# A hybrid attention and mLSTM layer: turned rows of q and k moved to GpSimd's DMA queue through DRAM, two separate scale broadcasts, softmax steps placed first, four split blocks of x kept in DRAM

## Chip, cores and metric

One core of one Trainium2 chip. The metric is the device time of one execution in microseconds (us). Before the change three executions took 2060.83, 2059.70 and 2060.79 us, median 2060.79 us. TensorE is called PE, VectorE DVE, ScalarE ACT, GpSimd POOL and SyncE SP, as in the profile.

## What is computed

```python
h = rmsnorm(x, norm_w); proj = h @ w_in            # x is 1024 x 2048, w_in 2048 x 9232, float32
q_a,k_a,v_a,z_a, q_m,k_m,v_m,o_m,z_m, g = split(proj)
# group A, 8 heads x 128: q and k are normalised (rmsnorm), their first 32 dims rotated,
# out[:, :16] = x1*cos - x2*sin, out[:, 16:32] = x2*cos + x1*sin
# three dilated windows (128,1), (512,4), (2048,16), mixed by their softmax denominators
attn = sum_p mix_p * softmax(q k^T / sqrt(128) + mask_p) v ; attn *= silu(z_a)
# group B, 4 heads, qk 128, v 256: chunkwise mLSTM forward and backward, summed, normalised
hm = sigmoid(o_m) * rmsnorm(h_fwd + h_bwd) * silu(z_m)
return x + concat(attn, hm) @ w_out
```

## The kernel before

**The products.** Every float32 operand is split into a high and a low part (`t_hi`, `t_lo` of x; `w_hi`, `w_lo` of the weights), and each product is three matmuls: high by high (L714), low by high (L716), high by low (L718); in the output projection they are L742, L743 and L744. The input projection is done by a Strassen-like scheme with seven products for a group of two 128-column weight tiles, two halves of the 1024 tokens and half of the 2048 inputs. The seven left operands, products 0 to 6, are sums of four quarter blocks of x (B11, B12, B22, B21), each 512 tokens by 512 inputs as 128 partitions x 2048 numbers, held split in `t_hi[:, n]` and `t_lo[:, n]`.

**The unit.** The program is written as units `u`. One unit is one product: 12 matmuls of 128 x 512. Units 0 to 447 are the input projection (64 groups of 7), units 448 to 575 the output projection. Every engine runs one loop over `u` and in each unit does, in order: the eviction of unit u-1 (DVE L1204 to L1217, ACT L969 and L974), the split of the weights of unit u+2 (ACT `w_hi` L961, DVE `w_lo` L1190), then whatever other work is placed at that unit, and last the sums of weight blocks (`s_tmp`, DVE L1225 to L1246). PE does the unit's product first, then the small matmuls that are placed there. All queues are in order, SP's too: a `wait_ge` on SP holds all loads and stores behind it.

**The blocks of x.** The x blocks are built three times, because the input half (1024 of the 2048 rows) changes: at unit 0 (half 0), around unit 105 (half 1) and around unit 329 (half 0 again). `BUILD_AT[2]` is unit 329. A build loads the four quarters (`x_block`, L390), ACT scales them with the norm weight (L983), DVE makes four sums (`t_one`, `t_three`, `t_two`, `t_four`, L1254 to L1272), and for each of the seven products ACT writes the high part (`t_high`, L1003) and DVE the low part (`t_low`, L1281). These come at offsets 1, 3, 4, 5, 6, 8 and 9 from `BUILD_AT[b]` for products 0, 2, 1, 3, 4, 6 and 5. The product n of the new half is first used in unit 336 + n.

**The attention heads.** Head h starts at `A_START[h]` = 357 + 18 h; `at` is the unit counted from there. A head's steps:

- at -4: SP loads q and k (`raw_a`, `raw_b`) from the projection's result in DRAM (`fin`).
- at 0 to 3: squares (ACT), column sums (PE L863), root and reciprocal; SP stores the scales to `rs_dram` (at 3).
- at 2: SP loads the 32 rotated rows of q and k once more as 128 partitions x 256 (`turn`, L531, eight transfers). at 4 and 5: DVE rotates them (`rotate`, L1531 to L1540; it signals `a_rot`).
- at 5 on SP: wait for the scales, then two broadcasts of them into `a_q` and `a_k` (L543, 512 KB each). at 5 and 6 on SP: wait for `a_rot`, then four transfers SBUF to SBUF that put the turned rows back into `raw_a` or `raw_b` (L550).
- at 6: SP loads z (L556). at 8: SP waits for the normalised q, then loads v into `raw_a` (L560).
- DVE: at 7 normalised q (`normed`, L1547), at 8 z times the row scale (L1581), at 9 normalised k, at 10 v times the row scale (L1584).
- at 10 to 21: eight softmax steps, each with scores on PE (L894), masking and minimum on DVE (`masked`, L1559, L1564), exponentials on ACT (L1092), reciprocal on DVE (L1570), normalisation on ACT (L1098), transposes on PE (L911), copies out of PSUM (ACT L1105, DVE L1620) and values (PE L925, L929).

The steps of one head from at 18 on lie in the same units as the first steps of the next head. Heads 5, 6 and 7 lie in the output projection, where DVE also adds the residual and frees the PSUM bank (`output`, L1635). In groups 48 to 63 the projection's results are added to what the first half left in DRAM, by POOL's accumulating DMAs (L364 to L376). POOL does nothing else after unit 39.

Of the kernel before, what the change touches and what calls it, by code (L numbers as in the profile page):

```python
# [7 lines left out]
F32 = mybir.dt.float32  # L8
# [83 lines left out]

def chunk_of(n):
    return n if n < TB else STEPS - 1 - n
# [14 lines left out]
def build_program(nc, xT, w_all, w_gates, vecs, norm_cols, m_cols, att_mask, rope, eye, tri, fin, part, y_dram, eps_dram, rows_dram, rs_dram,  # L109
                  outT):  # L110
    with ExitStack() as ctx:
# [85 lines left out]
        turn = [view(4096, 512), view(4608, 512)]  # L197
        eps_rows, qk_rs = tri_m[:, 0, :], tri_m[:, 1, :]
# [46 lines left out]
        b_in = [[sem(f"b_in{i}_{k}") for k in range(KP)] for i in (B11, B12, B22)]  # L245
        b21_in = sem("b21_in")
# [3 lines left out]
        tl_done = [sem(f"tl_done{n}") for n in range(PRODUCTS)]  # L250

# [12 lines left out]
        x_ss = sem("x_ss")  # L264
        x_rms = sem("x_rms")
        x_rs = sem("x_rs")
        x_cols = sem("x_cols")
        x_bc = sem("x_bc")
        x_norm = sem("x_norm")
        eps_out = sem("eps_out")  # L270
# [44 lines left out]
        bc_in = sem("bc_in")  # L315
        turn_in = [sem(f"turn_in{i}") for i in range(2)]
        a_rot = sem("a_rot")
# [9 lines left out]
        a_mh = sem("a_mh")  # L327
# [54 lines left out]
        def _(sp):  # L382
# [4 lines left out]
            def x_block(b, blk, kt):  # L387
# [3 lines left out]
                             ).then_inc(b21_in if blk == B21 else b_in[blk][kt], 16)  # L391
# [37 lines left out]
            def gate_stores(u):  # L429
                if u == 48:  # L430
                    sp.wait_ge(x_cols, 6)
                    sp.dma_start(eps_dram, spread1[0:2 * TB, 0, :]).then_inc(eps_out, 16)
# [4 lines left out]

            def build_loads(b, off):
                if off == -13:
                    if b == 1:  # L440
                        sp.wait_ge(g_pe, 1)
                        sp.wait_ge(rows_out, 64)
# [6 lines left out]
                for blk, at in ((B11, -13), (B12, -12), (B22, -11), (B21, -9)):  # L449
                    if off == at:  # L450
                        for kt in range(KP):
                            x_block(b, blk, kt)

            def mlstm_loads(j, at):
                g = M_FINAL[j]
                n, odd = divmod(at - 18, 2)
                if odd == 0 and 0 <= n < STEPS:
# [3 lines left out]
                    else:  # L461
                        sp.wait_ge(eps_out, 16)
                        sp.wait_ge(rows_out, 64)
# [40 lines left out]
            def attention_loads(h, at):  # L504
                g = A_FINAL[h]
                if at == -4:
                    if h == 0:
                        sp.wait_ge(tl_done[1], t_made(1, 2))
                        sp.wait_ge(tl_done[5], t_made(5, 2))
                        sp.wait_ge(tl_done[3], t_made(3, 2))  # L510
                        sp.wait_ge(tl_done[4], t_made(4, 2))
                        sp.wait_ge(tl_done[6], t_made(6, 2))
                        sp.wait_ge(m_t, 16 * M_HEADS)
                        sp.dma_start(eps_rows[0:2 * TB], eps_dram).then_inc(eps_out, 16)
# [1333 lines left out]
```

## Time and profile before

| | |
|---|---|
| median of three executions | 2060.79 us |
| the profiled execution's own time | 2060.51 us |
| its span, first to last instruction | 2058.4 us |
| PE busy | 1990.4 us, 97% of the span |
| DVE, ACT, POOL busy | 1300.3, 848.7, 174.0 us |
| DMA | 281.53 MB, mean 137 GB/s |
| mean granted TensorE clock | 0.993 |

The profile is one execution. Busy time of PE counts pipelined matmuls until their modelled end. "Idle before" a group is the engine's idle time just before its instructions, put down to what ended it. PEq and SPq are the sequencers.

### The profile page before, as it was taken

Reading aid. Unit: us, or ns where it says so; the run is one execution under the profiler, and the core shown is the slowest. Engines: PE = TensorE matmul, PEld = TensorE weight load, DVE = VectorE, ACT = ScalarE, POOL = GpSimd, SP = SyncE. Lnnn points to the kernel's source line nnn. Section 1 sums busy time; section 2 is a strip of 40 time slices with the busy share of each in tenths; the row PEclk is TensorE's granted clock in tenths of the full one; section 3 lists DMA queues with packets and bytes.
Section 4 is the critical chain, followed back from the end, with each engine's and each line's share of the span. In section 5 each row is a group of like instructions: output and inputs, shape, how many; then the busy total and the mean of one; then the engine's idle time right before and its main releaser. Section 6 shows DMA issues by size and latency. Waiting matters only on the chain.

```text
span 2058.4 us, 27134 instructions
## 1 busy us (share of the span) xinstructions
PE 1990.4 (97%) x9257; PEld 1626.8 (79%) x9257; DVE 1300.3 (63%) x2669; ACT 848.7 (41%) x1350; POOL 174.0 (8%) x156
## 2 busy tenths in 40 slices
PE   4999999999999999999998999999989999999999
PEld 3887788788888888888887878778777787778887
DVE  7777757768768768768778566575665544433222
ACT  5553325335335426335454253644536344242110
POOL 4340000110010010010000111010110000000000
PEclk9999999999999999999999999999999999999999
DMA  4552335564474465375354655364555625425443
GB/s 160 182 179 88 109 113 184 121 151 123 118 166 119 116 161 144 97 180 141 98 199 108 158 138 132 75 154 93 113 121 158 233 66 170 141 74 184 144 153 107
DMA packets 160551, 281.53 MB, mean 137 GB/s; under 512 B 18288, under 2 KB 39312, under 8 KB 160160
## 3 DMA queue, kind: packets, MB, share of 16 engines
q1 hardware_dynamic: 141984, 246.25, 37.3%
q0 software_dynamic: 18432, 33.56, 11.6%
q8 instruction: 75, 1.23, 0.2%
q14 instruction: 60, 0.49, 0.1%
HBM read 185.23 MB, written 92.41 MB: 135 GB/s over the span
## 4 chain that ended last, share of the span: by engine, by line
PE 87%; DVE 4%; issue 3%; ACT 2%; DMA 2%; SPq 1%; DVEq 0%; ACTq 0%
PE ps L714 18%; PE ps L718 18%; PE ps L716 18%; PE ps L742 5%; PE ps L743 5%; PE ps L744 5%; PE ps L925 3%; PE ps L894 2%; PE ps L863 1%; PE ps L819 1%; PE ps L828 1%; PE ps L911 1%; PE ps L822 1%; PE ps L929 1%; DVE w_lo L1190 1%
## 5 line engine op out<-in xcount | busy, mean ns | idle before, releaser
L714 PE MATMUL ps<-t_hi,w_hi 128*128 128x512 f32 x1792 | 717.5, 400 | 48.3 <-DVE t_lo L1644 12.4
L716 PE MATMUL ps<-t_lo,w_hi 128*128 128x512 f32 x1792 | 702.0, 392 | 0.0
L718 PE MATMUL ps<-t_hi,w_lo 128*128 128x512 f32 x1792 | 701.9, 392 | 0.0
L714 PEld LDWEIGHTS ps<-t_hi,w_hi 128*128 128x128 f32 x1792 | 338.8, 189 | 130.5 <-issue 64.1
L718 PEld LDWEIGHTS ps<-t_hi,w_lo 128*128 128x128 f32 x1792 | 338.7, 189 | 72.3
L716 PEld LDWEIGHTS ps<-t_lo,w_hi 128*128 128x128 f32 x1792 | 339.4, 189 | 65.8
L961 ACT CAST w_hi<-w_raw 128x512 fp32r<-128x512 f32 x256 | 158.4, 619 | 417.6 <-PE ps L718 200.8
L961 ACT CAST w_hi<-s_tmp 128x512 fp32r<-128x512 f32 x256 | 158.6, 620 | 268.2 <-PE ps L718 239.6
L1190 DVE TENSOR_TENSOR w_lo<-s_tmp,w_hi 128x512 fp32r<-128x512 f32 x256 | 182.3, 712 | 125.2 <-ACT w_hi L961 115.7
L1190 DVE TENSOR_TENSOR w_lo<-w_raw,w_hi 128x512 fp32r<-128x512 f32 x256 | 181.7, 710 | 119.9 <-ACT w_hi L961 113.5
L742 PE MATMUL ps<-t_hi,w_hi 128*128 128x512 f32 x384 | 155.7, 405 | 9.5 <-DVE xt L1635 9.5
L743 PE MATMUL ps<-t_lo,w_hi 128*128 128x512 f32 x384 | 151.4, 394 | 0.0
L744 PE MATMUL ps<-t_hi,w_lo 128*128 128x512 f32 x384 | 151.0, 393 | 0.0
L1635 DVE TENSOR_TENSOR xt<-ps,s_tmp 128x512 f32<-128x512 f32 x64 | 43.9, 687 | 142.8 <-PE ps L744 142.8
L364 POOL DMA_DIRECT2D fin_dram<-xt x32 | 27.8, 869 | 911.2 <-ACT xt L974 911.2
L742 PEld LDWEIGHTS ps<-t_hi,w_hi 128*128 128x128 f32 x384 | 73.3, 191 | 30.2 <-issue 15.9
L744 PEld LDWEIGHTS ps<-t_hi,w_lo 128*128 128x128 f32 x384 | 73.1, 190 | 15.9
L743 PEld LDWEIGHTS ps<-t_lo,w_hi 128*128 128x128 f32 x384 | 73.5, 191 | 14.0
L1054 ACT ACTIVATE arena<-arena,g_cols 128x128 f32<-128x128 f32 x64 | 25.8, 403 | 131.6 <-DVE arena L1427 131.6
L969 ACT COPY xt<-ps 128x512 f32<-128x512 f32 x64 | 37.6, 587 | 96.6 <-PE ps L718 96.5
L1092 ACT ACTIVATE arena<-arena,mins 128x704 f32<-128x704 f32 x64 | 56.6, 884 | 43.1 <-DVE mins L1564 43.0
L1098 ACT ACTIVATE arena<-arena,sums 128x704 f32<-128x704 f32 x64 | 56.4, 882 | 43.2 <-DVE sums L1570 43.2
(215 smaller groups left out, 2667.6 us busy)
## 6 DMA issues: line engine op xcount, KB each, us to landing
w_raw<-w_all_dram SPq DMA_DIRECT2D x320, 256.0 KB, 3.6
fin_dram<-xt SPq DMA_DIRECT2D x128, 256.0 KB, 4.2
fin_dram<-xt POOLq DMA_DIRECT2D x128, 256.0 KB, 4.5
arena<-fin_dram SPq DMA_DIRECT2D x64, 512.0 KB, 6.4
arena<-xT_dram SPq DMA_DIRECT2D x48, 256.0 KB, 5.8
arena<-xT_dram SPq DMA_DIRECT2D x16, 512.0 KB, 4.0
arena<-rs_dram SPq DMA_DIRECT2D x16, 512.0 KB, 5.9
y_raw<-y_dram SPq DMA_DIRECT2D x16, 512.0 KB, 5.1
```

Source lines behind the costliest of these rows:

```text
L714: nc.tensor.matmul(ps[:, bank, :], hi, t_hi[:, n, k, :], start=new and k == 0, stop=False, skip_group_check=True)
L716: nc.tensor.matmul(ps[:, bank, :], hi, t_lo[:, n, k, :], start=False, stop=False, skip_group_check=True)
L718: mm = nc.tensor.matmul(ps[:, bank, :], lo, t_hi[:, n, k, :], start=False, stop=k == KP - 1, skip_group_check=True)
L742: nc.tensor.matmul(ps[:, half, :], hi, yh, start=piece == 0 and k == 0, stop=False)
L743: nc.tensor.matmul(ps[:, half, :], hi, yl, start=False, stop=False)
L744: mm = nc.tensor.matmul(ps[:, half, :], lo, yh, start=False, stop=piece == 1 and k == KP - 1)
L925: nc.tensor.matmul(out, vtok[:, 4 * h + b, :], pT[:, b, :], start=b == 0, stop=False)
L961: nc.scalar.copy(w_hi[:, b % 3, :], src).then_inc(hi_done, 1)
L1092: nc.scalar.activation(prob[:, i % 2, 0:KEYS], prob[:, i % 2, 0:KEYS], ACT.Exp, bias=mins[:, i % 2:i % 2 + 1], scale=-1.0, accum_out=sums[ ...
L1098: nc.scalar.activation(prob[:, i % 2, 0:KEYS], prob[:, i % 2, 0:KEYS], ACT.Copy, scale=sums[:, 2 + i % 2:3 + i % 2]).then_inc(a_p, 1)
L1190: nc.vector.tensor_tensor(w_lo[:, b % 3, :], src, w_hi[:, b % 3, :].bitcast(F32), ALU.subtract).then_inc(lo_done, 1)
L1635: nc.vector.tensor_tensor(xt[:, e % 6, :], ps[:, e % 2, :], s_tmp[:, e % 3, :], ALU.add).then_inc(o_done, 1)
```

## The change

What it does, part by part:

1. **Turned rows.** The rotated rows of q and k are written to a new DRAM tensor `rot_dram` and read back into `raw_a` / `raw_b`, both on POOL's queue: one store (128 KB) and one load (128 KB) each for q and k instead of four SBUF-to-SBUF transfers on SP. POOL waits for `a_rot`, stores, and waits for the store's semaphore `rot_out` before it loads. The order of the 32 dims is interleaved (`TURNED`), so `turn` is loaded by four transfers instead of eight, and the shuffle mask becomes `r ^ 2`.
2. **Scales.** The broadcasts of q's and k's scales go out at 5 and at 6 with a semaphore each (`bc_in[i]`), and `normed` waits only for its own.
3. **v and z.** v gets a place of its own (`v_at`), its load moves from at 8 to at 4 and no longer waits for the normalised q. On DVE v is scaled at 7 (before: 10), q normalised at 8 (7), k at 9 (9), z scaled at 10 (8).
4. **Softmax steps first.** On DVE and ACT the head's softmax steps come at the start of a unit, ahead of the eviction and the weight split.
5. **Kept blocks.** Products 1, 3, 4 and 5 (`KEPT`) of the first build are stored to `t_dram` by SP in units 16 to 44 (eight stores of 1 MB) and loaded back in units 332 to 336 (eight loads of 1 MB). The third build then makes only products 0, 2 and 6: no load and no scaling of B12, none of the four sums, no high and low parts of the four.
6. **Semaphores.** B12, B22 and B21 wait for all four pieces of a quarter; several others are merged.

```diff
+KEPT = (1, 3, 4, 5)
+        v_at = view(5504, 1024)
 # SP
+            def t_stores(u):
+                i, rest = divmod(u - 16, 8)
+                if rest in (0, 4) and 0 <= i < len(KEPT):
+                    n = KEPT[i]
+                    sp.wait_ge(tl_done[n], t_made(n, 0))
+                    sp.dma_start(t_dram[i, rest // 4], flat_t((t_hi, t_lo)[rest // 4], n)).then_inc(t_out, 16)
+            def t_loads(u):
+                off = u - BUILD_AT[2]
+                if off - 2 in KEPT:
+                    n = off - 2
+                    i = KEPT.index(n)
+                    sp.wait_ge(prod, PRODUCTS * (STAGE[2] - 1) + n + 1)
+                    for part_, t in enumerate((t_hi, t_lo)):
+                        sp.dma_start(flat_t(t, n), t_dram[i, part_]).then_inc(t_in[i], 16)
-                    if off == at:
+                    if off == at and (b, blk) != (2, B12):
                         for kt in range(KP):
                             x_block(b, blk, kt)
-                if at == 5:
+                if at in (5, 6):
+                    i = at - 5
                     sp.wait_ge(rs_out, 32 * (h + 1))
                     sp.wait_ge(a_ss, h + 1)
-                    for i, to in enumerate((a_q, a_k)):
-                        sp.dma_start(to, rs_dram[h, i]...).then_inc(bc_in, 16)
-                if at in (5, 6):
-                    i = at - 5
-                    raw, to = ((raw_a, turn[0]), (raw_b, turn[1]))[i]
-                    sp.wait_ge(a_rot, 8 * h + 4 * i + 4)
-                    for k in range(4):
-                        sp.dma_start(raw[0:ROT, k * 256:(k + 1) * 256], to[k * ROT:(k + 1) * ROT, 0:256]
-                                     ).then_inc(turned[i], 16)
+                    sp.dma_start((a_q, a_k)[i], rs_dram[h, i]...).then_inc(bc_in[i], 16)
+                if at == 4:
+                    if h > 0:
+                        sp.wait_ge(a_pv, 4 * h)
+                    tile_done(sp, g[0], 0)
+                    sp.dma_start(halves(v_at), fin_tile(g[0], 0)).then_inc(v_raw, 16)
-                if at == 8:
-                    sp.wait_ge(a_rope, 2 * h + 1)
-                    tile_done(sp, g[0], 0)
-                    sp.dma_start(halves(raw_a), fin_tile(g[0], 0)).then_inc(v_raw, 16)
 # PE, in product(u)
-                if g in STAGE and not (g == 0 and n < 2):
+                if g == STAGE[2] and n in KEPT:
+                    pe.wait_ge(t_in[KEPT.index(n)], 32)
+                elif g in STAGE and not (g == 0 and n < 2):
                     pe.wait_ge(tl_done[n], t_made(n, STAGE.index(g)))
 # ACT and DVE: in build(), for b == 2 only products 0, 2 and 6, and no sums; in the loops
             for u in range(UNITS):
+                for h in range(ATT_HEADS):
+                    softmax_dve(h, u - A_START[h])      # ACT: softmax_act
                 if 1 <= u <= IN_UNITS:
                     evict(u - 1)
 # DVE
-                if at == 8:
+                if at == 10:
                     dve.wait_ge(z_raw, 16 * (h + 1))
-                if at == 10:
+                if at == 7:
                     dve.wait_ge(v_raw, 16 * (h + 1))
-                if at in (7, 9):
-                    normed(h, (at - 7) // 2)
+                if at in (8, 9):
+                    normed(h, at - 8)
 # POOL
+            def turned_rows(h, at):
+                if at in (4, 5):
+                    i = at - 4
+                    pool.wait_ge(a_rot, 8 * h + 4 * i + 4)
+                    pool.dma_start(rot_dram[h, i], turn[i][:, 0:256]).then_inc(rot_out[i], 16)
+                if at in (5, 6):
+                    i = at - 5
+                    pool.wait_ge(rot_out[i], 16 * (h + 1))
+                    pool.wait_ge(a_sq, 2 * h + 2)
+                    pool.dma_start(halves((raw_a, raw_b)[i][0:ROT]),
+                                   rot_dram[h, i].rearrange("(s r q) n -> r s (q n)", s=2, q=2)).then_inc(turned[i], 16)
             for u in range(UNITS):
                 if u <= IN_UNITS + 1:
                     g, n = divmod(u, PRODUCTS)
                     added(g, n) if g < NG or n < 2 else None
+                for h in range(ATT_HEADS):
+                    turned_rows(h, u - A_START[h])
```

## Rows read from the trace of the kernel before

**Rows 1.** The page: busy time of each engine.
```profile
PE 1990.4 (97%) x9257; PEld 1626.8 (79%) x9257; DVE 1300.3 (63%) x2669; ACT 848.7 (41%) x1350; POOL 174.0 (8%) x156
```

**Rows 2.** Waits of PE: who it waited for, total us, times, longest; then DVE's.
```profile
PE ps L742 <- DVE xt L1635: 9.5, 3, 4.2
PE ps L894 <- DVE mins L1564: 2.3, 3, 1.5
...
DVE arena L1547 <- DMA arena<-arena: 22.5, 4, 6.6
DVE arena L1581 <- DMA arena<-fin_dram: 11.1, 4, 3.6
```

**Rows 3.** Stretches of 18 units, heads 0 to 7: length, busy by engine, PEclk, DMA.
```profile
1163.00:1240.70 77.70, 74.95 (x371) 59.53 (x370) 49.65 (x118) 36.36 (x59) 8.64 (x10) 1.00 0.54 126
1240.70:1323.00 82.30, 82.17 (x413) 65.75 (x411) 52.27 (x128) 40.30 (x64) 9.50 (x11) 1.00 0.54 122
1323.00:1408.60 85.60, 82.74 (x413) 65.60 (x411) 53.49 (x132) 40.45 (x65) 8.44 (x10) 1.00 0.46 105
1408.60:1490.50 81.90, 81.90 (x413) 65.79 (x411) 52.07 (x128) 40.56 (x65) 8.83 (x11) 1.00 0.54 123
1490.50:1580.90 90.40, 84.60 (x413) 67.30 (x411) 54.94 (x129) 43.23 (x67) 8.66 (x10) 0.96 0.55 134
1580.90:1669.30 88.40, 83.92 (x413) 66.81 (x411) 47.05 (x116) 39.91 (x58) 1.73 (x2) 0.98 0.53 173
1669.30:1757.30 88.00, 83.79 (x414) 66.99 (x411) 39.15 (x106) 33.82 (x52) 0.00 (x0) 0.98 0.38 126
1757.30:1843.50 86.20, 83.64 (x413) 66.80 (x411) 39.14 (x107) 32.82 (x50) 0.00 (x0) 0.98 0.39 124
```

**Rows 4.** Eight units ahead of the third build, eight units in it; then two short stretches.
```profile
1060.70:1082.40 21.70, 21.70 (x97) 18.00 (x96) 18.13 (x30) 9.03 (x16) 0.00 (x0) 1.00 0.36 130
1082.40:1111.30 28.90, 23.19 (x98) 17.65 (x98) 25.09 (x28) 17.18 (x17) 0.00 (x0) 1.00 0.31 98
...
0.00:20.00 20.00, 5.17 (x12) 3.80 (x12) 11.29 (x25) 10.55 (x16) 3.06 (x5) 1.00 0.88 306
1518.00:1530.00 12.00, 11.15 (x50) 8.90 (x48) 4.46 (x8) 2.83 (x5) 1.34 (x2) 1.00 1.03 252
```

**Rows 5.** DVE in order of time, head 4: last rotation of k, normalised q.
```profile
1519.22 0.43 DVE L1540 TENSOR_TENSOR arena<-arena 128x256 f32<-128x256 f32 x1
1529.10 2.03 DVE L1547 SCALAR_TENSOR_TENSOR arena<-arena,spare 128x1024 f32<-128x1024 f32 x1 [6.60 <-DMA arena<-arena]
```

**Rows 6.** SP's queue in order of time, head 4, units at 5 and 6.
```profile
1518.13 0.85 SPq L543 DMA_DIRECT2D arena<-rs_dram  x2
1519.03 5.22 SPq L550 DMA_DIRECT2D arena<-arena  x8
```

**Rows 7.** PE in order of time: the first matmul of the unit at 5, head 4.
```profile
1515.39 0.39 PE L714 MATMUL ps<-t_hi,w_hi 128*128 128x512 f32 x1
```

**Rows 8.** Issue to landing, us min/median/max: L550, then L543, 1518 to 1526; L550, 1431 to 1440.
```profile
DMA to landing us min/median/max: 6.0/6.8/8.0
...
DMA to landing us min/median/max: 7.3/8.4/9.6
...
DMA to landing us min/median/max: 1.8/2.7/3.3
```

**Rows 9.** POOL's transfers, issue to landing, 1160 to 1590; then its issues of L372, ns.
```profile
DMA to landing us min/median/max: 3.8/4.2/8.1
L372 POOL DMA_DIRECT2D fin_dram<-xt x14: 862/864/865, 1161.4 to 1582.0; - x14
```

**Rows 10.** The page's DMA issues: count, KB each, median us to landing.
```profile
arena<-xT_dram SPq DMA_DIRECT2D x16, 512.0 KB, 4.0
y_dram<-arena SPq DMA_DIRECT2D x4, 1024.0 KB, 4.1
```

**Rows 11.** Groups of instructions of DVE, 1060.7 to 1111.3 (columns as in the page).
```profile
L1281 DVE TENSOR_TENSOR t_lo<-arena,t_hi 128x2048 fp32r<-128x2048 f32 x6 | 13.7, 2287 | 2.3 <-ACT t_hi L1003 2.3
```

More of the change, by code:

```diff
@@ L243, in build_program @@
         xa = [sem(f"xa{i}") for i in range(6)]
-        b_in = [[sem(f"b_in{i}_{k}") for k in range(KP)] for i in (B11, B12, B22)]
-        b21_in = sem("b21_in")
+        b11_in = [sem(f"b11_in{k}") for k in range(KP)]
+        b_in = {i: sem(f"b_in{i}") for i in (B12, B22, B21)}
         pre = [sem(f"pre{i}") for i in range(4)]
@@ L314, in build_program @@
         rs_out = sem("rs_out")
-        bc_in = sem("bc_in")
+        bc_in = [sem(f"bc_in{i}") for i in range(2)]
         turn_in = [sem(f"turn_in{i}") for i in range(2)]
+        rot_out = [sem(f"rot_out{i}") for i in range(2)]
         a_rot = sem("a_rot")
@@ L326, in build_program @@
         a_s = sem("a_s")
-        a_mh = sem("a_mh")
         a_m = sem("a_m")
@@ L1531, in rotate @@
                 nc.vector.memset(spare[:, 0:1], 0.0)
-                nc.vector.stream_shuffle(to[:, 256:512], to[:, 0:256], mask=[(r + ROT // 2) % ROT for r in range(ROT)]
+                nc.vector.stream_shuffle(to[:, 256:512], to[:, 0:256], mask=[r ^ 2 for r in range(ROT)]
                                          ).then_inc(a_rot, 1)
@@ L1735, in _ @@
                     added(g, n) if g < NG or n < 2 else None
+                for h in range(ATT_HEADS):
+                    turned_rows(h, u - A_START[h])
                 if u == 0:
@@ L1748 @@
 GD_COLS = GD_ROWS + 3
+TURNED = [i + s * (ROT // 2) for i in range(ROT // 2) for s in range(2)]
 def shape_constants():
@@ L1811 @@
     for h in range(ATT_HEADS):
-        cols += [a[:, P * h:P * (h + 1)] for a in (va, qa, ka, za)]
+        turned = [P * h + i for i in TURNED + list(range(ROT, P))]
+        cols += [va[:, P * h:P * (h + 1)], qa[:, turned], ka[:, turned], za[:, P * h:P * (h + 1)]]
     wo = w_out[0].reshape(2, D_MODEL // 2, D_MODEL)[::-1].reshape(D_MODEL, D_MODEL)
@@ L1819 @@
     for i, weight in enumerate((q_norm_w[0], k_norm_w[0])):
-        turned = weight[:ROT].reshape(2, ROT // 2)
         vecs[:ROT, i], vecs[ROT:, i] = 1.0, weight[ROT:]
-        vecs[:, 3 + 2 * i] = _np.tile(turned.reshape(ROT), 4)
-        vecs[:, 4 + 2 * i] = _np.tile(turned[::-1].reshape(ROT), 4)
+        own, other = weight[TURNED], weight[[(d + ROT // 2) % ROT for d in TURNED]]
+        vecs[:, 3 + 2 * i] = _np.tile(_np.repeat(own, 2), 2)
+        vecs[:, 4 + 2 * i] = _np.tile(_np.repeat(other, 2), 2)
     arrays = {
```

161 lines of the change are left out of this document (87 added, 74 removed).

## The prediction

> **What bounds the kernel now.** I read the page's busy times first [rows 1]: PE is busy 97% of the span, DVE 63%, ACT 41%. So an edit that only lightens DVE, ACT or SP is worth nothing by itself. It is worth something where PE waits, and PE's busy time, 1990.4 of 2058.4 us, leaves 68 us for that. The second view is PE's waits [rows 2]: behind the start, the waits are for DVE (the PSUM bank that `output` L1635 must free, 9.5 us, and the mask L1564, 2.3 us). DVE's own waits say why DVE is late: 22.5 us for the turned rows (DMA `arena<-arena` ahead of L1547) and 11.1 us for z (L1581).
>
> The third view puts a size on it [rows 3]. I cut the head phase into stretches of 18 units, one for a head, and the PE instruction counts (411 to 414 in heads 1 to 7) say that the stretches hold the same work. Head 3 takes 81.90 us and PE is busy through all of it. The others are longer than head 3 by 0.4 (head 1), 3.7 (2), 8.5 (4), 6.5 (5), 6.1 (6) and 4.3 us (7), together 29.5 us. Head 0 shares its units with no earlier head, so I take its idle PE time, 77.70 - 74.95 = 2.8 us. In all 32.3 us of the head phase are waits and their after-effects. The length shows more than the PE idle time does: in head 4 the idle time is 5.8 us and the stretch is 8.5 us too long, because the granted clock of that stretch fell to 0.96, that is, PE ran for a while at the lower of its two levels after it had stood still.
>
> The same comparison for the third build [rows 4]: eight units ahead of it take 21.70 us (2.71 us a unit), eight units in it 28.90 us. So 7.2 us are lost there, and DVE is busy 25.09 us of the 28.90, so here DVE's work itself is the limit. The first 54 us, the gate phase and the second build also have waits, and the change leaves their work as it is.
>
> **Turned rows, broadcasts, v and z (parts 1 to 3).** In head 4 the last rotation of k ends at 1519.22 + 0.43 = 1519.65 [rows 5]. SP issued the broadcasts at 1518.13 and the turned rows from 1519.03 on, 5.22 us for eight issues [rows 6]. They landed 6.0 to 8.0 us after issue, where in head 3 the same transfers took 1.8 to 3.3 us [rows 8]. The difference is the burst: from 1518 to 1530 the DMA share is 1.03, against 0.5 in the usual head [rows 3, 4]. DVE stood 6.60 us before normalised q [rows 5].
>
> After the change the path for k is: rotation end, POOL store, landing, POOL load, landing. No plain transfer on POOL stands in the trace. The nearest row is POOL's accumulating store of 256 KB: 4.2 us median from issue to landing, 3.8 to 8.1, of which 0.86 us is the issue [rows 9]. Two in a row make 8.4 us; from below, two of SP's fastest turned rows make 2 x 1.8 = 3.6 us [rows 8]; from above 2 x 8.1 = 16.2 us. I take 8.4 us in a quiet head, since issue and queue are the same, and about 12 us (twice the burst's 6.0) in a burst.
>
> What time is there? The unit at 5 starts at 1515.39 [rows 7], and rotation of k ends 4.3 us into it. Scores come behind the product of the unit at 10, six units of 2.71 us after that start, 16.3 us. Normalised k takes about 2.05 us [rows 5], so its rows are due 16.3 - 2.05 - 4.3 = 10.0 us after the rotation. So 8.4 us fits with 1.6 us to spare, and a burst's 12 us costs 2.0 us. For q the store goes out one unit earlier but its load stands on POOL behind k's store, so it is issued at about the same time as k's store ends, 0.9 us after k's rotation; it lands 4.2 us later and is due at 8, some 8.1 + 1.3 - 4.3 = 5.1 us after that rotation: 0.1 us over or under, which the slack of k takes up.
>
> On POOL, what stands behind a waiting turned row is an accumulating store of the result; it waits at most for the rotation, under one unit, and its `xt` buffer is asked for again a group (19 us) later, so that costs nothing. The scale broadcasts took 7.3 to 9.6 us in the burst [rows 8]; issued at the same moment, q's lands by 1525.4 and k's by 1528, near where DVE wants them (units at 8 and 9 start at 1523.5 and 1526.2, and DVE first has 1.2 us of weights and evictions). v goes out a unit ahead of the weights and has three units (8.1 us) before DVE scales it, for a 512 KB load of about 4.0 us [rows 10]. z keeps its place on SP but is wanted two units (5.4 us) later, more than its longest wait of 3.6 us [rows 2], so those waits go. SP no longer waits for `a_rot` and issues two transfers a head instead of eight, so the weights and residuals behind it go out earlier; this is what should free L1635 in heads 5 to 7.
>
> What comes anew: q and k are normalised in adjacent units. DVE's load in units 8 and 9 is then about 3.3 and 3.9 us (eviction, weights, 2.05, a sum), 7.2 us in 5.4. Laid out by hand from the start of unit 7 it ends in time for the scores in heads 0 to 4, and in heads 5 and 7 it puts `output` about 0.7 us late.
>
> What I leave in, head by head: 0.5, 0.3, 1.0, 0.5, 2.5, 2.2, 1.0 and 1.5 us, 9.5 us together (head 4 has the 2.0 us of the burst, heads 5 and 7 the 0.7 us, head 5 also its change to the output projection). Gain 32.3 - 9.5 = 22.8 us. Bounds: all 32.3 us go; or nothing goes and each head waits 16.2 - 10.0 = 6.2 us.
>
> At this place two rules of the Trainium skill speak against the edit. The page "DMA: Bandwidth & Descriptors", section "SWDGE vs HWDGE vs iDMA", says that transfers issued from GpSimd on one side and from SP on the other run on the same 16 engines and interleave, so another issuer saves only issue time. The burst rows agree: POOL's own stores reach 8.1 us. By it the turned rows gain nothing in a burst; that is the second rival below. The same section says that GpSimd writes its descriptors into SBUF and that DVE can lock it out of there in one of its modes. No row here shows that: POOL's issue takes 862 to 865 ns beside a DVE that is busy 60% of the time, so by the rule the sum would grow and by the row it does not.
>
> **Softmax steps first (part 4).** PE's three waits for the mask are 2.3 us [rows 2] and are inside the 32.3. The eviction of unit u-1 now stands behind the mask, some 1.9 us later, and its bank is wanted only when unit u+1 starts, 4.7 us or more after unit u in these units; the weights of unit u+2 have more. I count no loss; if that cover were gone it would be some 0.5 us a step.
>
> **Kept blocks (part 5).** DVE loses in the third build four low parts of 2.29 us [rows 11] and 16 sums of a quarter of that width (some 0.6 to 0.7 us each), together about 20 us; ACT loses as many scalings and high parts. Three low parts stay, each alone, and each is longer than what DVE has to spare in a unit ((21.70 - 18.13) / 8 = 0.45 us) [rows 4]. I leave 0.5 us for each of them, 1.4 us in all, so 5.8 of the 7.2 us would go [rows 4].
>
> Against this stand the loads: eight of 1.05 MB. The start of the run moved 306 GB/s at a share of 0.88 [rows 4], 348 GB/s if full, so 8.4 MB take 24 us of the engines. They can't start before product 1 of the group before is done, about 1085.5, and product 5 is used first in unit 341, at about 1082.4 + 11 x 2.71 + 1.4 = 1113.6. That leaves 28 us, in which the usual traffic takes a share of 0.31 [rows 4], 9 us. 24 + 9 = 33 us and a landing of some 1 us more: product 5 would be up to 5 us late, products 1, 3 and 4 in time. If the weights of that group go out behind it, it is 0. I take 2 us. The part gives 5.8 - 2.0 = 3.8 us; bounds 5.8 and, at the 252 GB/s of the burst [rows 4] for everything, 33 + 9 us against 28, a wait of 14 us and a loss of 8.
>
> The eight stores at units 16 to 44 lie one in four units. A store of 1 MB lands after 4.1 us, a load of x there after 4.0 us [rows 10], and SP issues the next load of x a good 5 us behind the store. No PE wait stands in that stretch, so I count 0; bounds -0 and 8 x 1 us if each load of x behind a store is late.
>
> **Semaphores and start (part 6).** Waiting for four pieces instead of one touches the start, where ACT scales B12 while DVE is still three steps behind it: 0, at most 1 us.
>
> **Sum.** 2060.5 (the profiled execution's own time; its span is 2058.4, so 2.1 us lie around it) - 22.8 - 3.8 = 2033.9. The profiled execution is 0.3 us below the median of the three, 2060.8, so I keep the sum: **2034 us**. Its own range is 2027 to 2041.
>
> **Rivals.**
> - *Everything goes.* All 32.3 us and all 5.8 us: 2060.5 - 38.1 = 2022.4. For it: head 3 shows a head without a wait. Against: DVE's two adjacent normalisations and head 4's burst.
> - *The burst stays.* The turned rows pay 12 us instead of 8.4 in every head, 2.0 us each, 16 us instead of 9.5: 2040.4. For it: the burst is made of weights and broadcasts, which stay. Against: heads 1 and 3 had no such burst.
> - *The kept blocks are late.* The build ends 8 us slower instead of 3.8 faster: 2033.9 + 11.8 = 2045.7. For it: four transfers of 2.1 MB stand on the queue that also brings weights. Against: 1 MB stores land in 4.1 us.
> - *Slower.* GpSimd's round trip through DRAM is longer than its slack in every head. If both landings are like the longest one, 16.2 us, each head stands 6.2 us, 49.6 us in place of 32.3: 2060.5 + 17.3 - 3.8 = 2074. It turns into a loss against before from a round trip of 10.0 + 36.1 / 8 = 14.5 us on. For it: POOL's 8.1 us. Against: the median of 4.2.
> - *It does not do what it says.* The waits stay because something else that lands at the same time releases DVE, such as k's broadcast: about 2058 to 2061.
>
> **How the numbers follow.** Forecast 0.52, everything goes 0.12, burst stays 0.18, kept blocks late 0.10, slower 0.06, no effect 0.02. A measurement of this kernel tells 0.2%, 4 us, from no change. Only the last two lie above 2057, with a tail of the kept blocks: faster 0.90, same 0.03, slower 0.07. The range 2022 to 2048 holds the first four and leaves out the last two and the edge of the first, between one and two in ten.
>
> **What would show it.** Right: DVE's wait before normalised q and the L1581 wait gone; stretches of 18 units all between 81.9 and 84.5 us; POOL's turned rows landing 3 to 5 us after issue; the eight units of the third build at about 25 us with any PE wait put down to a DMA into `t_hi` or `t_lo`. Wrong: a DVE wait for `arena<-rot_dram`, or scores that wait for normalised k in quiet heads (the slack of 10.0 us was misjudged); PE waits of over 5 us at unit 340 or 341; PE waits for evictions in the softmax units; longer units between 16 and 44.

## The result, and the profile after

The changed kernel takes **2039.12 us** (median of four runs, 2035.74 to 2043.08), the kernel before took 2060.24 us beside it (2057.34 to 2060.83). The ratio is 0.9904, with a 95% interval of 0.9885 to 0.9924: faster by 21 us, or 1%. Forecast were 2034 us in a range of 2022 to 2048. The profiled execution took 2038.74 us with a span of 2036.9 us and a mean granted clock of 0.996.

The page's busy times, beside [rows 1]:
```profile
PE 1984.6 (97%) x9257; PEld 1623.8 (80%) x9257; DVE 1282.5 (63%) x2649; ACT 837.5 (41%) x1342; POOL 192.6 (9%) x188
```
DVE and ACT have lost the work of the third build, 18 and 11 us. PE executes the same 9257 matmuls and is 5.8 us less busy: matmuls at the lower clock level last longer, and fewer of them now run at it.

Cutting both traces at PE's first matmul of a unit says where the 21.5 us of the span went:

| units | what is there | before | after | difference | forecast |
|---|---|---|---|---|---|
| 0 to 16 | start | 69.1 | 69.1 | 0 | 0 |
| 16 to 48 | stores of the kept blocks | 100.8 | 100.8 | 0 | 0 |
| 48 to 116 | gates, second build | 198.3 | 198.3 | 0 | 0 |
| 116 to 316 | products, mLSTM | 661.7 | 660.0 | -1.7 | 0 |
| 330 to 338 | third build | 28.8 | 23.2 | -5.6 | -5.8 |
| 338 to 346 | first products of the new half | 21.8 | 23.9 | +2.1 | +2.0 |
| 357 to 501 | the eight heads | 680.5 | 664.2 | -16.3 | -22.8 |
| 501 to 575 | rest of the output projection | 208.8 | 208.8 | 0 | 0 |

The 1.7 us of units 116 to 316 are not the change's: e7 and e10 below, which have all of it that acts there, show 661.6 us, and e9, which has no kept blocks and touches the heads only from unit 362 on, shows 660.3.

The stretches of 18 units of the eight heads, which answer to [rows 3] (start and end, length, busy times of PE, PEld, DVE, ACT, POOL, clock, DMA share, GB/s), and below them two short stretches around the turned rows of heads 5 and 6:
```profile
1157.80:1234.00 76.20, 75.03 (x372) 59.76 (x371) 48.21 (x116) 35.41 (x58) 11.03 (x14) 1.00 0.54 129
1234.00:1315.90 81.90, 81.90 (x413) 65.84 (x411) 52.92 (x130) 40.48 (x64) 11.80 (x15) 1.00 0.56 128
1315.90:1398.90 83.00, 82.62 (x413) 65.73 (x411) 52.42 (x129) 40.40 (x65) 10.18 (x13) 1.00 0.46 112
1398.90:1480.80 81.90, 81.90 (x413) 65.82 (x411) 51.82 (x128) 40.15 (x65) 11.96 (x15) 1.00 0.54 126
1480.80:1567.10 86.30, 83.79 (x414) 66.93 (x411) 55.68 (x131) 43.17 (x68) 11.06 (x14) 0.98 0.56 143
1567.10:1653.70 86.60, 82.65 (x413) 65.60 (x411) 47.24 (x115) 39.10 (x57) 3.94 (x6) 1.00 0.55 174
1653.70:1735.80 82.10, 82.08 (x413) 65.88 (x411) 39.51 (x108) 34.32 (x52) 2.24 (x4) 1.00 0.43 145
1735.80:1822.00 86.20, 83.88 (x412) 66.55 (x410) 39.17 (x107) 32.48 (x50) 2.25 (x4) 0.98 0.37 120
1591.00:1607.00 16.00, 14.46 (x64) 11.66 (x64) 8.15 (x14) 2.52 (x3) 2.15 (x4) 1.00 1.01 339
1677.00:1692.00 15.00, 15.00 (x68) 12.43 (x67) 7.36 (x13) 2.53 (x3) 2.24 (x4) 1.00 1.03 347
```
Heads 1, 3 and 6 now run without loss. Heads 4, 5 and 7 are still 4.3 to 4.7 us too long. The average DMA share of a head is about 0.5, which hides what the short stretches show: while the turned rows of heads 5 and 6 travel, the 16 DMA engines are full.

The waits, which answer to [rows 2]; POOL's own wait between its two transfers, DVE's waits for the turned rows and for v, PE's waits for DVE, and the wait for a kept block:
```profile
POOL arena L1776 <- DMA rot_dram<-arena: 32.0, 12, 5.7
DVE arena L1576 <- DMA arena<-rot_dram: 25.0, 10, 6.1
...
DVE arena L1624 <- DMA arena<-fin_dram: 3.1, 3, 1.5
...
PE ps L760 <- DVE xt L1668: 5.4, 3, 2.2
...
PE ps L732 <- DVE xt L1232: 4.0, 4, 2.5
...
PE ps L732 <- DMA t_lo<-t_dram: 1.1, 1, 1.1
...
PE ps L911 <- DVE mins L1593: 0.3, 1, 0.3
```
DVE's wait for z (11.1 us before) is gone; a smaller one for v (L1624, 3.1 us in heads 5 to 7) is new. PE's wait for the mask fell from 2.3 to 0.3 us. DVE's wait for the turned rows did not fall: 22.5 us before, 25.0 us now, with other names.

What such a wait does is seen in head 4, in order of time. First DVE, then POOL, then PE (start, duration, line, in brackets the idle time before and what ended it):
```profile
1518.54 2.05 DVE L1576 SCALAR_TENSOR_TENSOR arena<-arena,spare 128x1024 f32<-128x1024 f32 x1 [2.62 <-DMA arena<-rot_dram]
1520.52 0.68 DVE L1249 TENSOR_TENSOR s_tmp<-w_raw 128x512 f32<-128x512 f32 x1
1521.12 0.68 DVE L1232 TENSOR_TENSOR xt<-ps,xt 128x512 f32<-128x512 f32 x1
1521.72 0.68 DVE L1214 TENSOR_TENSOR w_lo<-s_tmp,w_hi 128x512 fp32r<-128x512 f32 x1
1522.72 2.07 DVE L1576 SCALAR_TENSOR_TENSOR arena<-arena,vec 128x1024 f32<-128x1024 f32 x1 [0.33 <-DMA arena<-rot_dram]
```
```profile
1510.22 0.57 POOL L1771 DMA_DIRECT2D rot_dram<-arena  x1 [2.10 <-DVE arena L1569]
1510.78 0.58 POOL L1776 DMA_DIRECT2D arena<-rot_dram  x1
1511.35 0.94 POOL L380 DMA_DIRECT2D fin_dram<-xt  x1
1517.97 0.57 POOL L1776 DMA_DIRECT2D arena<-rot_dram  x1 [5.68 <-DMA rot_dram<-arena]
```
```profile
1521.94 0.47 PE L732 MATMUL ps<-t_hi,w_hi 128*128 128x512 f32 x1 [2.51 <-DVE xt L1232]
...
1523.19 0.63 PE L734 MATMUL ps<-t_lo,w_hi 128*128 128x512 f32 x1
```
Normalised q (the first L1576) waits for its rows. Behind it on DVE stands the eviction L1232, and PE's next product needs that bank. PE stands 2.51 us, and after it PE's matmuls take 0.63 us in place of 0.39 for 3 us, that is, the lower clock level. It is q, not k, on which DVE stands: 2.62, 6.13 and 5.92 us in heads 4, 5 and 7, against 0.33, 1.44 and 1.16 us for k.

### The profile page after: what moved, and what is told of

Read it like the earlier page. It is cut to its first block, busy times and chain, and to the rows that moved or that the text cites. A ratio compares the mean times of both kernels' runs of the same rounds, so it can differ in the third digit from the quotient of the medians.

```text
span 2036.9 us, 27050 instructions
## 1 busy us (share of the span) xinstructions
PE 1984.6 (97%) x9257; PEld 1623.8 (80%) x9257; DVE 1282.5 (63%) x2649; ACT 837.5 (41%) x1342; POOL 192.6 (9%) x188
## 4 chain that ended last, share of the span: by engine, by line
PE 88%; DVE 4%; DMA 3%; issue 3%; ACT 1%; SPq 0%; POOL 0%; DVEq 0%; ACTq 0%; POOLq 0%
PE ps L732 18%; PE ps L734 18%; PE ps L736 18%; PE ps L760 5%; PE ps L762 5%; PE ps L761 5%; PE ps L942 3%; PE ps L911 3%; PE ps L880 1%; PE ps L836 1%; PE ps L845 1%; PE ps L928 1%; DMA arena<-rot_dram 1%; PE ps L839 1%; PE ps L946 1%
## 5 line engine op out<-in xcount | busy, mean ns | idle before, releaser
L1668 DVE TENSOR_TENSOR xt<-ps,s_tmp 128x512 f32<-128x512 f32 x64 | 44.0, 687 | 140.3 <-PE ps L762 140.3
L761 PEld LDWEIGHTS ps<-t_lo,w_hi 128*128 128x128 f32 x384 | 72.5, 189 | 13.8
```

Source lines behind the costliest of these rows:

```text
L761: nc.tensor.matmul(ps[:, half, :], hi, yl, start=False, stop=False)
```

## The experiments

The heads' sum is the stretch of units 357 to 501 of the profiled run; without any loss it would be 74.5 + 7 x 81.9 = 647.8 us (the shortest head 0 and the shortest other head that any run shows). "Before" was measured beside each, on three chips: 2060.38 us for e1, e2, e3 and e5, 2061.48 us for e6 to e9, 2061.69 us for e10 and e11. So medians from different chips can differ by about 1 us with nothing changed; the ratios are each to their own "before". Each number of the heads is that of one profiled execution. Summary:

| run | median us | ratio, 95% | heads | units 330 to 338, 338 to 346 |
|---|---|---|---|---|
| before | 2060.24 | | 680.5 | 28.8, 21.8 |
| the change | 2039.12 | 0.9885 to 0.9924 | 664.2 | 23.2, 23.9 |
| e1 kept blocks only | 2058.49 | 0.9974 to 0.9998 | 681.9 | 23.2, 26.5 |
| e2 without kept blocks | 2044.06 | 0.9892 to 0.9934 | 663.2 | 28.8, 21.8 |
| e3 turned rows on SP | 2030.59 | 0.9829 to 0.9874 | 652.0 | 23.2, 24.8 |
| e5 one hop on GpSimd | 2027.77 | 0.9817 to 0.9855 | 649.3 | 23.2, 23.4 |
| e6 short broadcasts | 2037.42 | one run | 661.0 | 23.2, 23.2 |
| e7 e5, old places | 2054.51 | 0.9949 to 0.9977 | 679.0 | 23.2, 23.1 |
| e8 e5, softmax late | 2033.40 | 0.9852 to 0.9888 | 654.7 | 23.2, 28.7 |
| e9 before, own broadcast | 2056.64 | 0.9972 to 0.9993 | 676.7 | 28.8, 21.8 |
| e10 thin traffic | 2026.15 | one run | 650.3 | 23.2, 23.8 |
| e11 e5, no kept blocks | 2028.96 | 0.9827 to 0.9860 | 650.5 | 28.8, 21.8 |

**e1: the kernel before with the kept blocks alone** (and the loads' semaphores merged).
```diff
+KEPT = (1, 3, 4, 5)
+                    t_stores(u)
+                    t_loads(u)
```


> The kernel before with the kept blocks alone (products 1, 3, 4, 5 stored and loaded back), and the merged load semaphores that make room for its own. The theory from the two traces: the part is worth 5.6 us in the eight units from 330 and gives 2.1 us back in the eight behind them, where the product that is loaded last waits for its transfer, so the whole is 3.5 us faster than before, about 2056.7 us, with the head phase (units 357 to 501) at 680.5 us as before. Rival: the stores and loads of 1 MB disturb the rest, and the part alone is no faster than before; or the 5.6 us belong to the new order of DVE's steps and not to the blocks, and units 330 to 338 stay at 28.8 us.

Measured: 5.6 us gained in the build as forecast, 4.8 us given back in units 338 to 346, where the product loaded last waits for its transfer. The run is faster than before by 1.9 us, where 3.5 were expected, and its interval only just leaves 1 out. The heads are what they were.

**e2: the changed kernel without the kept blocks.**
```diff
-KEPT = (1, 3, 4, 5)
+KEPT = ()
 ... (B12 is loaded and the sums are made again in the third build)
```


> The changed kernel with the third build made in full as before, nothing kept. The theory: 3.5 us slower than the changed kernel, about 2042.6 us; units 330 to 338 at 28.8 us, 338 to 346 at 21.8, heads at 664.2 as changed. Rival: parts interact, for instance the loads delay the heads' transfers, and this is not slower than the changed kernel.

Measured: the build is back at 28.8 and 21.8 us, the heads stay at 663.2. So the gain of the heads does not depend on the kept blocks, and the heads make most of the gain.

**e3: the turned rows back on SP, SBUF to SBUF**, each set behind its own broadcast; places, softmax steps and kept blocks as changed.
```diff
 # SP, behind each broadcast; POOL's turned_rows is taken out
+                    sp.wait_ge(a_rot, 8 * h + 4 * i + 4)
+                    for k in range(4):
+                        sp.dma_start((raw_a, raw_b)[i][0:ROT, k * 256:(k + 1) * 256],
+                                     turn[i][k // 2 * 64 + k % 2:k // 2 * 64 + 64:2, 0:256]).then_inc(turned[i], 16)
```


> The changed kernel with the turned rows put back on SP: after each broadcast SP waits for the rotation and issues four transfers SBUF to SBUF, nothing through DRAM and nothing on GpSimd. Theory A (the gain of the heads comes from taking the turned rows off SP): the rows land behind the broadcasts and SP is held again, units 357 to 501 take about 674 us (660 would be without any wait, 680.5 before), the time is about 2049. Theory B (the gain comes from the later place of normalised q and from the early v): 664 us or less for the heads, 2039 or less in all.

Measured: 2030.59 us, heads 652.0. I had expected the waits to come back; the run is 8.5 us faster than the change instead. My reason that SP must be freed of these transfers fell. (The 660 us "without any wait" of my expectation was too high: it is 647.8.)

**e5: one hop.** The same four SBUF-to-SBUF transfers, but on GpSimd's queue.
```diff
-                    pool.dma_start(rot_dram[h, i], turn[i][:, 0:256]).then_inc(rot_out[i], 16)
 ... (the load from rot_dram and its two waits are taken out too)
+                    pool.wait_ge(a_ss, h + 1)
+                    for k in range(4):
+                        pool.dma_start((raw_a, raw_b)[i][0:ROT, k * 256:(k + 1) * 256],
+                                       turn[i][k // 2 * 64 + k % 2:k // 2 * 64 + 64:2, 0:256]).then_inc(turned[i], 16)
```


> The changed kernel with one hop: GpSimd's queue moves the turned rows SBUF to SBUF, four transfers each for q and k, without the way through DRAM. Theory A (what is left in heads 4 to 7 is two lengthened landings in a row, 12.8 to 14.2 us against 10.0 allowed): one landing of 5 to 8 us and four issues of some 0.6 us fit, the heads take 650 to 654 us instead of 664.2, in all about 2027. Theory B (what is left is the burst, whoever carries the rows, and the small pieces and eight issues on GpSimd eat the gain): 662 us or more for the heads, 2038 or more in all.

Measured: 2027.77 us, heads 649.3, 1.5 us above a head phase without any loss. It is 11.4 us faster than the change, and it beats both kernels. Heads 5 to 7 of this run, and the short stretch around head 5's turned rows:
```profile
1563.50:1646.30 82.80, 82.06 (x413) 65.72 (x411) 47.23 (x115) 39.10 (x57) 5.92 (x10) 1.00 0.55 179
1646.30:1728.20 81.90, 81.90 (x413) 65.84 (x411) 39.49 (x108) 34.34 (x52) 4.12 (x8) 1.00 0.41 142
1728.20:1810.10 81.90, 81.90 (x414) 65.84 (x411) 39.23 (x107) 32.52 (x50) 4.12 (x8) 1.00 0.37 123
1587.00:1603.00 16.00, 16.00 (x72) 13.24 (x71) 11.99 (x18) 2.53 (x3) 4.21 (x8) 1.00 1.02 344
```
The engines are as full as in the changed kernel (1.02 against 1.01), and each transfer is as slow. Issue to landing of its 64 transfers of 32 KB, min, median and max, and what DVE still waits for at normalised q and k:
```profile
L1773 POOL DMA_DIRECT2D arena<-arena x64: 522/523/687, 1179.5 to 1755.6; - x64
...
DMA to landing us min/median/max: 1.8/5.2/7.5
```
```profile
DVE arena L1576 <- DMA arena<-arena: 3.2, 2, 1.6
DVE arena L1576 <- DMA arena<-rs_dram: 2.3, 2, 1.6
```
So here full engines cost almost nothing when the rows cross them once: heads 6 and 7 lose nothing, and head 5 loses 0.9 us.

**e6: short broadcasts.** The changed kernel, with 128 of 1024 columns of the scales brought.
```diff
+                    sp.dma_start((a_q, a_k)[i][:, 0:128], rs_dram[h, i].rearrange("r b n -> (r b n)")[0:128].unsqueeze(0)
+                                 .to_broadcast([P, 128])).then_inc(bc_in[i], 16)
```


> The changed kernel, but each broadcast of the scales brings only the first 128 of 1024 columns, 64 KB instead of 512; the rest of the scales is left out. It keeps GpSimd's round trip through DRAM. Theory A (the two hops are slow because the broadcasts and other traffic of SP fill the engines): the stores and loads of the turned rows land 2.5 to 4 us after issue in every head, the heads (units 357 to 501) fall from 664.2 to about 650 us, in all about 2025. Theory B (the round trip is slow by itself, whatever else moves): landings of 5 to 8 us stay in heads 5 to 7 and the heads take 660 or more.

Measured: heads 661.0, only 3.2 us less. The share at the turned rows of heads 5, 6 and 7 was still 0.96, 1.00 and 0.83 with the broadcasts nearly gone, and the turned rows still took 5 to 8 us each. These are theory B's numbers, but they don't show its reason, that the trip is slow by itself: the engines were still full. The broadcasts alone are not what fills them; e10 takes the other traffic away too.

**e7: e5 with DVE's old places**: q at 7, z at 8, k at 9, v at 10.
```diff
-                if at == 10:
+                if at == 8:
                     dve.wait_ge(z_raw, 16 * (h + 1))
-                if at == 7:
+                if at == 10:
                     dve.wait_ge(v_raw, 16 * (h + 1))
-                if at in (8, 9):
-                    normed(h, at - 8)
+                if at in (7, 9):
+                    normed(h, (at - 7) // 2)
```


> The one-hop kernel (GpSimd's queue, SBUF to SBUF, 2027.8 us, heads 649.3) with the old places on VectorE: q normalised at 7, z scaled at 8, k at 9, v at 10. Theory A (what carries most of the gain is that the rows are wanted a unit later, 2.7 us for q, and z two units later): heads 4 to 7 wait again, 2 to 3 us each, and the heads take 656 to 664 us, in all 2035 to 2043. Theory B (taking the rows off SP is enough): 651 or less, 2029 or less.

Measured: 2054.51 us, heads 679.0: 29.7 us of the heads come back (26.7 us in the medians), all but 1.5 us of what the kernel before had. That is more than theory A expected (656 to 664). DVE's waits for transfers in e7, beside those of e5 above:
```profile
DVE arena L1621 <- DMA arena<-fin_dram: 14.5, 5, 6.6
DVE arena L1576 <- DMA arena<-arena: 13.9, 5, 4.8
DVE arena L1576 <- DMA arena<-rs_dram: 8.1, 2, 4.7
```
z's wait (L1621) is 14.5 us, more than the 11.1 us of before; e5 has none, though it waits 4.5 us for v. The 6.6 us are in head 2, whose stretch is:
```profile
1320.20:1410.60 90.40, 85.16 (x414) 67.77 (x411) 52.48 (x129) 40.36 (x65) 12.17 (x17) 0.96 0.41 100
```
That wait of DVE's and the lower clock after PE's stop (0.96 in the mean) make the head 8.5 us too long.

**e8: e5 with the softmax steps back behind eviction and weights.**
```diff
-                for h in range(ATT_HEADS):
-                    softmax_dve(h, u - A_START[h])
 ...
                 for h in range(ATT_HEADS):
+                    softmax_dve(h, u - A_START[h])
                     attention_dve(h, u - A_START[h])
 ... (ACT likewise, behind attention_act)
```


> The one-hop kernel with the softmax steps back behind the eviction and the weight split on VectorE and ScalarE. Theory A: TensorE waits again for the mask and the copies out of PSUM, as in the rows of before (2.3 us and its after-effects): heads 652 to 654 us instead of 649.3, in all about 2031. Theory B: with the turned rows in time VectorE is never late and the order is worth nothing: 649 to 650, 2028.

Measured: heads 654.7, 5.4 us more than e5; the median is 5.6 us above e5's. PE's waits of this run name the mask again, with the 2.3 us that it had before the change, a copy out of PSUM on ACT (in the same head e5 has a wait of 0.7 us for ACT's normalisation instead), and its one wait for a kept block:
```profile
PE ps L732 <- DMA t_lo<-t_dram: 3.2, 1, 3.2
PE ps L911 <- DVE mins L1592: 2.3, 3, 1.3
PE ps L928 <- ACT arena L1125: 1.8, 1, 1.8
```
The granted clock is 1.00 in all eight heads of e8, so the clock is no part of the 5.4 us; some 2 us of them stand in no wait of PE that the profile lists, and stay open. The 7.0 us lost in units 338 to 346 of this profile (PE's stop of 3.2 us and a mean clock of 0.88 there) are the kept load's: an edit in the heads can't reach them, so they show how much that wait varies from run to run (1.3 to 7.0 us over eight profiles that have the kept blocks).

**e9: the kernel before, each broadcast followed by its own turned rows.**
```diff
-                if at == 5:
-                    for i, to in enumerate((a_q, a_k)):
-                        sp.dma_start(to, rs_dram[h, i]...).then_inc(bc_in, 16)
                 if at in (5, 6):
+                    sp.dma_start((a_q, a_k)[i], rs_dram[h, i]...).then_inc(bc_in[i], 16)
```


> The kernel before with one edit (and the merged load semaphores that make room): SP issues q's broadcast, then q's turned rows at 5, k's broadcast and k's turned rows at 6; q's normalisation waits for q's broadcast alone. Places on VectorE and everything else as before. Theory: q's turned rows no longer stand behind k's broadcast (2.7 us in head 4), so of the 32.3 us of the heads 10 to 15 go: heads 666 to 670, in all 2046 to 2050. Rival: SP now waits for the rotation ahead of k's broadcast, k comes later by what q gains, heads 678 or more, 2058 or more.

Measured: 2056.64 us, heads 676.7. The split of the broadcasts is worth 3.8 us in the heads by itself (4.8 us in the medians), between the two expectations. DVE's waits of this run say why it is no more:
```profile
DVE arena L1579 <- DMA arena<-fin_dram: 23.9, 7, 5.9
DVE arena L1545 <- DMA arena<-arena: 11.0, 4, 4.1
```
Normalised q and k (L1545) wait half as long as in [rows 2], 11.0 against 22.5 us. DVE then comes to z (L1579) earlier, and z's wait grows from 11.1 to 23.9 us. The one wait had covered part of the other.

**e10: thin traffic.** The changed kernel, two hops, with fewer bytes around it on SP.
```diff
+                n = 128 if g >= 51 else 512         # weights of the input projection
+                sp.dma_start(w_raw[:, slot, 0:128], w_all[tile * PIECES + piece][:, 0:128]).then_inc(w_in[slot], 16)
 ... (the broadcasts as in e6)
+                    sp.dma_start(halves(v_at)[:, :, 0:64], fin_tile(g[0], 0)[:, :, 0:64]).then_inc(v_raw, 16)
+                    sp.dma_start(halves(ystage)[:, :, 0:64], fin_tile(g[1], 1)[:, :, 0:64]).then_inc(z_raw, 16)
```


> The changed kernel, its trip through DRAM kept, with SP's traffic around a head's start thinned: the scale broadcasts bring 128 of 1024 columns, the loads of v and z 128 of 1024, the weight loads from group 51 on (unit 357) 128 of 512 columns. The rest of these operands is left out, so the output isn't the reference's; every instruction, wait and queue stays. Theory A (k's trip of 12.8 to 14.2 us in heads 4 to 7 is long because SP's transfers fill the DMA engines, and is 6.4 to 8.5 us where they don't): the trip is 6 to 9 us in every head, the heads take 648 to 653 us against 664.2, the span is 2021 to 2027. Theory B (the trip is long of itself in the output projection: two transfers of 128 KB in turn on GpSimd's queue and a wait between them, whatever SP does): the trip stays at 12 us or more in heads 4 to 7 and the heads take 660 us or more, as with the short broadcasts alone (661.0).

Measured: heads 650.3, span 2024.4. k's trip takes 7.4, 5.7, 7.5, 7.1, 7.2, 10.7, 10.4 and 9.7 us in heads 0 to 7. Heads 5 to 7 are a little over the 6 to 9 us expected, and their stretches still have shares of 0.6 to 0.8. Head 5's:
```profile
1586.00:1602.00 16.00, 15.61 (x70) 12.64 (x69) 10.83 (x17) 2.53 (x3) 1.98 (x4) 1.00 0.82 268
```
With the same instructions and waits, 13.9 of the 16.4 us that the change's heads still lose go away with the bytes alone. So the two hops are slow because of SP's other traffic, which fills the engines. Which of weights, v and z matters most was not tried.

**e11: e5 without the kept blocks.**
```diff
-KEPT = (1, 3, 4, 5)
+KEPT = ()
 ... (as in e2)
```


> The changed kernel with the turned rows in one hop on GpSimd's queue (the experiment that took 2027.8), and without the kept blocks: the third build makes all seven products again. Theory A (the kept blocks are worth the 5.6 us of units 330 to 338 less what product 5's wait for its load gives back in units 338 to 346, 1.6 us there, and nothing elsewhere): units 330 to 338 take 28.8, 338 to 346 take 21.8, heads 649 to 650, median 2031 to 2033, slower by 3 to 5 us. Theory B (the eight stores and eight loads of 1 MB cost as much elsewhere as they save): median 2026 to 2029, the same.

Measured: 2028.96 us, 1.2 us above e5, with intervals that overlap: the median is theory B's, while the parts of the profile are theory A's. In the profiles the build costs 5.6 us more, units 338 to 346 cost 1.6 us less and the heads 1.2 us more, but e5's first 16 units took 72.3 us and e11's 69.1. The start takes 69.1 or about 72 in different profiles with the kept blocks (four and four), and 69.1 in all four without them. Whether the blocks cause that can't be told from so few. Three pairs of medians price the kept blocks at 1.9 (e1), 4.9 (e2) and 1.2 us (e11, whose pair was measured on two chips). By the profiles they gain 5.6 us and give 1.3 to 7.0 back. They are worth 0 to 5 us, and that is all that these runs tell.

## Why the prediction held, and where it was off

**Third build, stores, mask: right in the profile.** The build gained 5.6 us (forecast 5.8), its last product waited for its load and lost 2.1 (2.0), together -3.5 against -3.8. The price of the late load was right for this profile only: it is 1.3 to 7.0 us from run to run, so that the agreement is in part luck. The eight stores cost nothing, 100.8 us before and after. Putting the softmax steps first did no harm, and e8 prices it at 5.4 us, more than the 2.3 us of PE's waits for the mask that I saw. A longer wait for ACT is 1.0 us of the difference; the rest is open.

**The heads: direction right, size and mechanism off.** 16.3 us gained, 22.8 forecast. The term that was mis-sized is "what I leave in": 9.5 us forecast, 16.4 us measured (664.2 - 647.8). And the wait that was to go did not: DVE stood 22.5 us for the turned rows before and 25.0 us after. A sign that I had set for being wrong is there, DVE's wait for `arena<-rot_dram`; PE waits for evictions behind it; and three heads take 86.2 to 86.6 us, not 84.5 at most. The time was inside the range because the order on DVE, of which I had made one reason among several, carried the gain.

**The round trip's time.** I took 8.4 us in a quiet head and 12 us in a burst, and charged the burst to head 4 alone. From the end of k's rotation (L1569) to its rows' landing the trace shows

| head | 0 | 1 | 2 | 3 | 4 | 5 | 6 | 7 |
|---|---|---|---|---|---|---|---|---|
| k's rows, us | 9.5 | 6.4 | 10.8 | 8.5 | 12.8 | 13.8 | 13.2 | 14.2 |
| q's rows, us | 10.9 | 9.1 | 7.8 | 8.7 | 12.2 | 12.0 | 13.0 | 12.7 |

For k the 8.4 us were a good size and the 12 us a little short. What was wrong is how many heads have a burst: I compared the stretch of 12 us in head 4 (share 1.03, [rows 4]) with the averages of whole heads (0.5, [rows 3]). I should have asked for the same short stretch in every head: after the change the share there is 0.85 to 1.03 in all eight. The trace before would have told: while its turned rows travelled, the share was 0.96, 1.04, 0.84, 0.88 and 0.95 in heads 0, 2, 5, 6 and 7, and heads 1 and 3, with 0.65 and 0.80, were the quietest. Heads 2 and 7 of the kernel before:
```profile
1348.60:1360.00 11.40, 11.40 (x52) 9.45 (x51) 8.62 (x15) 3.55 (x7) 1.88 (x3) 1.00 1.04 274
1781.30:1791.20 9.90, 9.90 (x45) 8.19 (x44) 4.71 (x7) 1.25 (x2) 0.00 (x0) 1.00 0.95 282
```
Head 3 after the change, the one that I had held for quiet:
```profile
1424.00:1436.00 12.00, 12.00 (x55) 9.93 (x54) 11.82 (x20) 3.53 (x6) 5.02 (x7) 1.00 0.86 240
```
A share of 0.86 leaves a trip of 8.5 us there; at 0.97 to 1.03 it takes 9.5 to 14.2 us (heads 0, 2, 5, 6 and 7), but 12.8 us in head 4 at 0.85, so the share tells that a trip may be long and not how long.
With the burst charged to heads 4 to 7 and not to head 4 alone, the sum would have come close to my second rival's, 2040.4 us, which is the nearest of all cases to the 2039.1 measured. That this rival comes so near is luck all the same: it charges 2.0 us for k to every head, while heads 4, 5 and 7 lose 4.3 to 4.7 us, mostly through q, and heads 1, 3 and 6 next to nothing. That the burst makes the trip long rests on e10: with the bytes gone, the trip is 5.7 to 7.5 us in heads 0 to 4 and 9.7 to 10.7 us in heads 5 to 7.

**The deadline.** I wrote of q's rows "0.1 us over or under, which the slack of k takes up", charged them no burst, and took the loss from the scores that follow normalised k. The runs show another limit. On DVE an eviction that frees PE's next bank stands behind the step that waits for q's rows, and k's slack is no help to it. In heads 4, 5 and 7 DVE stands 2.6, 6.1 and 5.9 us for q, and it is an eviction (L1232, L1668) that PE waits for. The trace before has this too, in a wait of PE that [rows 2] leaves out:
```profile
PE ps L714 <- DVE xt L1208: 7.1, 4, 5.7
```
Its 5.7 us are in head 4, behind DVE's 6.60 us of [rows 5]: the eviction L1208 came late.

How long DVE may stand for q differs. In head 4 its 2.6 us cost PE 2.5 us. In head 6 it stands 4.2 us and the stretch loses 0.2 us. In head 7 of e10 it stands
```profile
1760.01 2.05 DVE L1577 SCALAR_TENSOR_TENSOR arena<-arena,spare 128x1024 f32<-128x1024 f32 x1 [4.81 <-DMA arena<-rot_dram]
```
and the stretch loses 0.3 us. So q's rows are due when the eviction behind them can just still be in time: in head 4 as soon as DVE reaches the step, in heads 6 and 7 some 4 us later. In heads 5 to 7 k's rotation ends 0.6 to 0.7 us into the unit at 5, not 4.3 us as in head 4, so by my own sum k had 13.6 us there, not 10.0, and a trip of 13 to 14 us would have cost next to nothing.

**The reason for the gain.** I put it down to several edits at once, taking the rows off SP's queue among them. e3 and e5 differ in just that queue and differ by 2.7 us in the heads; e7, rows off SP but in the old places, leaves 31.2 us of loss. The order on DVE carries it: with q a unit later, z two units later and v, whose load has been out since 4, in the gap, 29.7 us go. The places were moved together; what each is worth was not tried. The trip through DRAM is a loss inside the change, 664.2 - 649.3 = 14.9 us in the heads.

At this point the Trainium skill's rule ("DMA: Bandwidth & Descriptors", section "SWDGE vs HWDGE vs iDMA"), that the transfers of GpSimd and SP share the same 16 engines and interleave, is what the runs agree with: at shares of about 1.0 the turned rows on GpSimd's queue landed after 5 to 8 us, as SP's did before the change (6.0 to 8.0 us, [rows 8]). I had this rule and applied it to a burst in one head only.

**The rivals.** "Everything goes" (2022.4) needed a trip that fits: e5, with one hop, got to 2027.8. "No effect" and "slower" stayed away; the longest trips (14.2 us for k, 13.0 for q) came within 0.3 us of the 14.5 us from which I had put a loss, and the kernel was still 21 us faster, for the threshold assumed that trip in every head and the wrong deadline for k.

## What to carry to other kernels

When a wait is caused by a transfer, look at the DMA share of the few microseconds in which it travels, in every repetition of the pattern, and not at the mean of the stage. Where the engines are full there, another queue changes little (2.7 us here); what counts is how often the data cross them and how long before their use they set out. And take as the deadline of a step on an in-order engine the work that stands behind it: ahead of a step that waits, place one whose data come earlier (here v, for which DVE waited 3.1 us in all). Moving four steps by up to three units was worth 29.7 us in the profiled heads and 26.7 us in the medians, the softmax steps about 5, the kept blocks 0 to 5.

## What the runs showed of the hardware

A small transfer was hardly quicker than a large one in full engines: in heads 5 to 7 the 24 transfers of 32 KB of e5 had a median of 5.8 us from issue to landing, the 12 of 128 KB of the changed kernel 6.1 us. Over all heads, the 32 KB transfers of e5, SBUF to SBUF, had a median of 5.2 us and up to 7.5 us, against 1.8 us at the least; those of 128 KB in the changed kernel ranged from 2.5 to 8.1 us around 5.3.

A stop of PE cost more than its length, with or without a lower clock. After PE's 2.5 us in head 4, its matmuls of 128 x 512 took 0.63 us each for about 3 us and then 0.39 again, and the stretch was 4.4 us longer than head 3's. In head 6, where DVE waited 4.2 us but PE never stopped, the clock stayed at 1.00 and the stretch lost 0.2 us. In head 4 of e3 PE stopped for 1.3 and 0.3 us, the clock stayed at 1.00, and the stretch was 2.1 us too long.

GpSimd issues a plain store or load of 128 KB in 0.57 us, one of 32 KB in 0.52 us, and the accumulating ones of 256 KB in 0.86 us [rows 9], while DVE is busy for 45 to 65% of the time beside it.
